# Two blocks on one core: the scan's keys on GpSimd, the residuals on VectorE, and the first feed-forward's output token-major

## The reference, cut to what matters

```python
def step(state, inp):                     # per head, chunkwise
    b = jnp.cumsum(gc, axis=2)
    o_inter = einsum('bhtk,bhkv->bhtv', qc * exp(b), state)
    decay = exp(minimum(b[:, :, :, None, :] - b[:, :, None, :, :], 0.0)) * mask
    scores = einsum('bhtk,bhsk,bhtsk->bhts', qc, kc, decay)
    o_intra = einsum('bhts,bhsv->bhtv', scores, vc)
...
x = x + rms_norm(mix, norm_mix_post[l])
h2 = rms_norm(x, norm_ffn_pre[l])
ff = (silu(h2 @ w_gate) * (h2 @ w_up)) @ w_down          # 2816 hidden
x = x + rms_norm(ff, norm_ffn_post[l])
x = x + (p[l] @ w_ple) * sigmoid(x @ w_ple_gate)
```

## Time and profile before

| what | value |
|---|---|
| median of 3 runs | 925.89 us (925.7 to 927.39) |
| the profiled execution's own time | 928.56 us |
| its span, first to last instruction | 926.7 us |
| mean granted TensorE clock | 0.978 |
| busy: PE / DVE / ACT / POOL | 95% / 64% / 48% / 5% of the span |
| read from memory | 141.87 MB |

### The profile page before, as it was taken

One profiled execution on the slowest core, in us unless ns is written; L12 is line 12 of the kernel. 1 busy time (PEld: TensorE's weight loads), 2 busy tenths in 40 slices (PEclk: granted clock), 3 DMA queues, 4 the chain that ended last, 5 costly groups with the idle time before them and its releaser, 6 DMA issues. The chain is left out here.

```text
span 926.7 us, 15775 instructions
## 1 busy us (share of the span) xinstructions
PE 882.5 (95%) x6990; PEld 860.9 (93%) x6990; DVE 597.2 (64%) x717; ACT 449.3 (48%) x524; POOL 44.4 (5%) x47
## 2 busy tenths in 40 slices
PE   5999989899999989999999999989996899999998
PEld 4999977899999989999999989988996899999997
DVE  5866975697576577555555577676776665555554
ACT  6577744345343664434343554464553644444441
POOL 1000000000000020000000021000342000000000
PEclk9999999899999999999999999998998999999999
DMA  9544323144445535555555526542231255555551
GB/s 341 195 152 168 122 105 136 46 139 139 144 141 181 184 132 182 182 182 182 182 183 183 181 95 229 168 157 95 92 119 60 91 182 182 182 182 182 182 183 46
DMA packets 21124, 143.94 MB, mean 155 GB/s; under 512 B 2579, under 2 KB 2595, under 8 KB 4417
## 3 DMA queue, kind: packets, MB, share of 16 engines
q1 hardware_dynamic: 20016, 139.51, 43.5%
q0 software_dynamic: 1040, 3.43, 1.1%
HBM read 141.87 MB, written 1.06 MB: 154 GB/s over the span
## 5 line engine op out<-in xcount | busy, mean ns | idle before, releaser
L1470 PE MATMUL ps<-xh,whi 128*128 128x256 f32 x1960 | 563.6, 288 | 18.3 <-issue 6.8
L1471 PE MATMUL ps<-xl,whi 128*128 128x256 f32 x1960 | 558.6, 285 | 0.0
L1472 PE MATMUL ps<-xh,wlo 128*128 128x256 f32 x1960 | 558.4, 285 | 0.0
L1470 PEld LDWEIGHTS ps<-xh,whi 128*128 128x128 f32 x1960 | 380.2, 194 | 21.9 <-issue 20.3
L790 DVE TENSOR_TENSOR wlo<-raw,whi 128x2048 fp32r<-128x2048 f32 x130 | 297.4, 2290 | 129.6 <-ACT whi L391 128.8
L1471 PEld LDWEIGHTS ps<-xl,whi 128*128 128x128 f32 x1960 | 380.2, 194 | 0.0
L1472 PEld LDWEIGHTS ps<-xh,wlo 128*128 128x128 f32 x1960 | 380.1, 194 | 0.0
L391 ACT ACTIVATE whi<-raw 128x2048 fp32r<-128x2048 f32 x130 | 247.9, 1908 | 163.6 <-DMA raw<-w 163.4
L574 ACT ACTIVATE xh<-work 128x512 fp32r<-128x512 f32 x27 | 17.1, 632 | 75.9 <-DVE work L1096 39.8
L1625 PE MATMUL ps<-work 128*128 128x128 f32 x224 | 32.3, 303 | 8.3 <-ACT work L471 8.3
L1625 PEld LDWEIGHTS ps<-work 128*128 128x128 f32 x224 | 30.2, 210 | 10.0 <-ACT work L471 9.9
(11 more groups left out here) (242 smaller groups left out, 666.3 us busy)
## 6 DMA issues: line engine op xcount, KB each, us to landing
raw<-w SPq DMA_DIRECT2D x130, 1024.0 KB, 4.9
x<-xT SPq DMA_DIRECT2D x2, 512.0 KB, 6.4
raw<-w SPq DMA_DIRECT2D x2, 512.0 KB, 7.5
work<-bias_scratch POOLq DMA_DIRECT2D x1, 1024.0 KB, 6.2
out<-x SPq DMA_DIRECT2D x4, 256.0 KB, 2.3
work<-lnr POOLq DMA_DIRECT2D x1, 512.0 KB, 6.0
work<-sgw POOLq DMA_DIRECT2D x1, 512.0 KB, 6.7
lvl_s<-lvl POOLq DMA_DIRECT2D x1, 448.0 KB, 8.3
```

The lines of the kernel that those rows point to most:

```text
L1470: mm(out, hi, xh[:, tile, :], start=start, stop=False, skip_group_check=skip)
L1471: mm(out, hi, xl[:, tile, :], start=False, stop=False, skip_group_check=skip)
L1472: return mm(out, wlo[:, slot, at:at + width], xh[:, tile, :], start=False, stop=stop, skip_group_check=skip)
```

## The change

The steps of the scan are put in two tables, `inside` (between the two halves of a unit) and `behind` (after a unit). K's half of `tree_update` goes to GpSimd as `keys_update`; ScalarE's copy waits for it. GpSimd's residual additions go to VectorE. `first_unit` makes the products with xh as soon as xh is there, and those with xl after. The down units of the first feed-forward accumulate token-major; their norm is taken per token (ScalarE's accumulated squares, factor by a power on GpSimd, a diagonal matrix on VectorE), and a product with that diagonal scales and turns them back to channels; VectorE adds them with the gain to x in one operation a tile. The folds, statistics and broadcast of n4 go.

```diff
 def hgrn_schedule():
-    steps = {}
-    for g, first in enumerate((10, 18)):
-        for lv in range(9):
-            steps.setdefault(first + lv, []).append(("level", g, lv))
-    for g, u in enumerate((19, 27)):
-        steps.setdefault(u, []).insert(0, ("pv", g, 0))
-    return steps
+    inside = {11: [("level", 0, 0)], 20: [("pv", 0, 0)], 28: [("pv", 1, 0)]}
+    behind = {18: [("level", 0, 8), ("level", 1, 0)], 27: [("level", 1, 8)]}
+    for lv in range(1, 8):
+        behind[10 + lv] = [("level", 0, lv)]
+        behind[19 + lv] = [("level", 1, lv)]
+    return inside, behind
...
 # GpSimd, ahead of the load of pT
+            def keys_update(g, lv):
+                half = 1 << (lv - 1)
+                n = 4 * T // (2 * half)
+                if lv == 1:
+                    pool.wait_ge(sem(f"q_init{g}"), 2)
+                else:
+                    pool.wait_ge(sem(f"decay{g}"), 2 * lv - 2)
+                pool.wait_ge(sem("Kc"), 7 * g + lv)
+                for d in range(2):
+                    pair = decay(g, d, lv - 1).rearrange("p (n two) -> p n two", two=2)
+                    v = G[g]["K"][d].rearrange("p h (n two w) -> p (h n) two w", two=2, w=half)[:, :, d, :]
+                    ins = nc.gpsimd.tensor_tensor(v, v, pair[:, :, 1 - d:2 - d].broadcast_to([P, n, half]), ALU.mult)
...
+                ins.then_inc(sem(f"ktree{g}"), 1)
+            for g in range(2):
+                for lv in range(1, 8):
+                    keys_update(g, lv)
...
-            for k in range(1, 4):
-                residual("n2", k)
...
-            for k in range(1, 4):
-                residual("ff", k)
...
+            for t in range(2):
+                pool.wait_ge(sem("ff_eps"), t + 1)
+                nc.gpsimd.tensor_tensor(fffac[:, t:t + 1], ffvar[:, t:t + 1], half_s[:, 0:1], ALU.pow).then_inc(sem("ff_fac"), 1)
...
 # ScalarE
                 if lv > 1:
-                    act.wait_ge(sem(f"tree{g}"), lv - 1)
+                    act.wait_ge(sem(f"ktree{g}"), lv - 1)
+                    act.wait_ge(sem(f"lv_mm{g}"), lv)
...
                 if kind == "pv":
                     act.wait_ge(sem(f"pv_mm{g}"), 1)
+                    if g == 0:
+                        both_ways(1, 1)
...
-                ahead(u)
+                if not U_ZI <= u < U_GA:
+                    ahead(u)
...
                             evac(u - 1 + s, zi[:, s, half * 512:half * 512 + 512], ACT.Copy, scale=rtok[:, 0, s:s + 1])
+                    ahead(u)
...
-                A(sq2[:, 2 * b:2 * b + 2, :], two(ps[3 + b][:, :]), ACT.Square).then_inc(sem("norm_sq"), 1)
-                for t in range(2):
-                    ins = A(mix[:, 2 * b + t, :], ps[3 + b][:, t * T:(t + 1) * T], ACT.Copy, scale=col("ffn_post", 2 * b + t))
-                ins.then_inc(sem("ff_copy"), 1)
+                A(ysq[:, b, :], ps[3 + b][:, :], ACT.Square, accum_out=ffsum[:, b:b + 1]).then_inc(sem("norm_sq"), 1)
...
 # VectorE, tree_update: Q alone, then the decays of the next level, each with a signal
+                for d in range(2):
+                    v = G[g]["Q"][d].rearrange("p h (n two w) -> p (h n) two w", two=2, w=half)[:, :, 1 - d, :]
+                    last = V.tensor_tensor(v, v, pairs[d][:, :, d:d + 1].broadcast_to([P, n, half]), ALU.mult)
...
-                if U_Q[0] <= u < U_ZI and (u - 4) % 6 == 5:
-                    gates((u - 4) // 6, 1, 1)
-                    if u < U_Q[1]:
-                        hgrn_dve("prep", 0, 0)
-                for step in steps.get(u, ()):
+                if u == U_Q[1] - 1:
+                    gates(0, 1, 1)
+                    hgrn_dve("prep", 0, 0)
+                for step in behind.get(u, ()):
                     hgrn_dve(*step)
                 ahead(u)
+                if u == U_ZI - 1:
+                    gates(1, 1, 1)
...
 # VectorE, n2
-                if k == 0:
-                    dve.wait_ge(sem("n2_y"), 1)
-                    V.tensor_tensor(x[:, t, :], x[:, t, :], tmp2[:, t, :], ALU.add).then_inc(sem("n2_x"), 1)
-                if k >= 2:
-                    gained_lo("n3", "ffn_pre", 8, k - 2)
-            gained_lo("n3", "ffn_pre", 8, 2)
+                dve.wait_ge(sem("n2_y"), k + 1)
+                V.tensor_tensor(x[:, t, :], x[:, t, :], tmp2[:, t, :], ALU.add).then_inc(sem("n2_x"), 1)
+                if k:
+                    gained_lo("n3", "ffn_pre", 8, k - 1)
...
 # VectorE, n4
+            def token_copy(b):
+                dve.wait_ge(sem("norm_sq"), before("sq", "n4") + b + 1)
+                V.tensor_copy(ytok[:, b // 2, (b % 2) * 512:(b % 2 + 1) * 512], ps[3 + b][:, :]).then_inc(sem("ff_copy"), 1)
+            def token_mean(t):
+                dve.wait_ge(sem("norm_sq"), before("sq", "n4") + 2 * t + 2)
+                link(V.tensor_tensor(ffvar[:, t:t + 1], ffsum[:, 2 * t:2 * t + 1], ffsum[:, 2 * t + 1:2 * t + 2], ALU.add))
+                V.tensor_scalar(ffvar[:, t:t + 1], ffvar[:, t:t + 1], 1.0 / D, EPS, ALU.mult, ALU.add).then_inc(sem("ff_eps"), 1)
+            def token_diag(t):
+                dve.wait_ge(sem("ff_fac"), t + 1)
+                V.tensor_scalar(diag[:, t, :], ident, fffac[:, t:t + 1], None, ALU.mult).then_inc(sem("ff_diag"), 1)
+            def token_residual(m):
+                if m % 2 == 0:
+                    dve.wait_ge(sem("ff_turned"), m // 2 + 1)
+                V.scalar_tensor_tensor(x[:, m, :], ps[TURNED[m // 2]][:, (m % 2) * T:(m % 2 + 1) * T], col("ffn_post", m),
+                                       x[:, m, :], ALU.mult, ALU.add).then_inc(sem("ff_x"), 1)
+            token_copy(0); token_mean(0); token_copy(1); token_diag(0)
+            token_copy(2); token_mean(1); token_copy(3); token_diag(1)
+            for k in range(4):
+                token_residual(2 * k)
+                token_residual(2 * k + 1)
+                if k:
+                    x_lo(k - 1)
+            x_lo(3)
...
 # TensorE, first_unit
+                for pair in range(4):
+                    blocks = [(m, k) for k in (2 * pair, 2 * pair + 1) for m in range(2)]
+                    pe.wait_ge(sem("act_hi"), before("hi", x_name) + pair + 1)
...
+                    pe.wait_ge(sem("act_lo"), before("lo", x_name) + pair + 1)
...
 # TensorE, the first feed-forward's output
+            def token_down(slot, base, s, c, kk, first, end):
+                xs = slice(s * P, (s + 1) * P)
+                wc = slice(1024 * kk + 512 * c, 1024 * kk + 512 * c + 512)
+                o = ps[3 + 2 * s + c][:, :]
+                mm(o, xh[:, base + kk, xs], whi[:, slot, wc], start=first, stop=False, skip_group_check=True)
+                mm(o, xl[:, base + kk, xs], whi[:, slot, wc], start=False, stop=False, skip_group_check=True)
+                return mm(o, xh[:, base + kk, xs], wlo[:, slot, wc], start=False, stop=end, skip_group_check=True)
...
-            last_down((U_PG - 1) % SLOTS, 2 * ((PAIRS1 - 1) % 2), "ff_bank")
-            idle_products(0, 14)
-            norm_stats("n4", sq2)
-            idle_products(0, 5)
-            norm_bc("n4")
-            idle_products(0, 9)
...
+            def turned(s, m):
+                return mm(ps[TURNED[m // 2]][:, (m % 2) * T + s * P:(m % 2) * T + (s + 1) * P], ytok[:, s, m * P:(m + 1) * P],
+                          diag[:, s, :], start=True, stop=True)
+            pe.wait_ge(sem("ff_copy"), 2)
+            pe.wait_ge(sem("ff_diag"), 1)
+            for m in range(8):
+                turned(0, m)
+            idle_products(2, 5)
+            pe.wait_ge(sem("ff_copy"), 4)
+            pe.wait_ge(sem("ff_diag"), 2)
+            for m in range(8):
+                last = turned(1, m)
+                if m % 2:
+                    last.then_inc(sem("ff_turned"), 1)
+            idle_products(2, 6)
```

151 lines of the change are left out of this document (74 added, 77 removed).

## The result

The changed kernel takes **902.2 us** (median of 4 runs, 900.72 to 903.32) against 926.64 for the kernel before on the same chip: ratio 0.9714, 95% interval 0.9683 to 0.9745, so 2.9% faster. Its profiled execution took 901.93 (span 900.1, mean granted clock 0.988), that of before 928.56 (926.7, 0.978).

The account below looks back on a forecast made before the run. TensorE, busy 95% of the span, was taken as the bound. Gains 16 + 3.5 + 5.5 + 1.5 + 0.9 = 27.4 us off the profiled 928.56 gave 901.2, as a median 898.5 us, range 893 to 909.

Parts of the forecast that it names:

- Parts 1 and 2: Scan: reordered levels, copies and splits, plus key updates moved to GpSimd, gain 16 us (bounds: 19.6, loss of about 4).
- 19.6 us lost: Scan: its 153.9 us less a sum of 134.3 us at TensorE's pace, taken as the time lost.
- Key updates at 1.48: Scan: GpSimd's price per key update, taken from its residual additions; at most one hold of VectorE per level.
- one of my own signs for "wrong": Scan: levels over 7.6 us apart (units 20-26), key updates over 2 us, or VectorE's times up over 20 us in all.
- Part 3: First feed-forward: eleven token-major down units at 5.43 instead of 5.77 us, gain 3.5 us (bounds 3 and 4.5).
- Part 4: Tail of the first feed-forward: shorter chain from last down product to next unit, gain 5.5 us (3.5 to 6.5).
- Part 5: Second residual and first_unit: gain 1.5 us (0 to 2) at the second norm, 0.9 us at the sixth.
- (a): Scan: shared port holds VectorE a second time in about half of levels 2-7; gain 6, median 908.5; chance 0.17.
- (b): Scan: both key updates of every level hold VectorE through the shared port, about 929 us; chance 0.05.
- (c): First feed-forward: token-major pays only 0.8 us instead of 3.5, median 901; chance 0.05.
- (d): Feed-forward tail: diagonal and turned products arrive no earlier, gain 0 instead of 5.5, median 904; chance 0.06.
- (e): Scan: another engine, ScalarE's queue in units 12 to 15, paces it as before; within 2 us of 925.9; chance 0.02.

Follow-up runs that it names:

- the second comparison: The changed kernel itself, unedited, run a second time beside the kernel before on the same chip: 901.0 us, ratio 0.9703.
- the run with the waits out: Changed kernel with ScalarE's first copies, VectorE's first group-1 query products and the last hidden products reordered to remove three waits: 898.62 us.
- the channel-major run: Changed kernel with the first feed-forward's down projections, norm and residual as before; scan and attention output residual as changed: 908.31 us.
- The doubled keys: Changed kernel with each GpSimd key update followed by a second in-place operation of the same shape (times one): 908.42 us.

## Why the prediction was right

It said 898.5 with 893 to 909, faster; it came to 902.2. By medians the gain is 24.4 us here (926.64 to 902.2) and 27.3 in the second comparison (928.31 to 901.0), for a forecast of 27.4. By its steps:

- **Parts 1 and 2**, gain 16: measured 14.4, and 15.0 in the second profile. The waits at level 6 and ahead of (1,1) went as said, (0,8) was 0.5 late where I had said 1. About 3.7 of the 14.4 are clock (an estimate: before, level (0,6) and the unit behind it took 1.4 and 0.3 us longer with part of them at clock 0.5, (1,1) and its unit 0.9 and 1.1). The "19.6 us lost" was too high: with unit 28 its sum at pace is 140.1, and the run with the waits out, where TensorE never waits, took 143.48. The sum left out 2.0 us of the longer first and second tree levels and the 0.08 us that each first product behind a level takes more (0.20 for 0.12, 0.31 for 0.23). So 17.1 could be had, and the 3.5 us that the prediction left standing are about this floor. What is missing up to 17.1 is the 0.5 at (0,8) and a wait that I hadn't seen, at (0,1): 2.1 us behind one activation on ScalarE. I looked for what stood behind ScalarE's new waits, not at what its copies stood behind.
- **Key updates at 1.48**: median 1.52, mean 2.00, so one of my own signs for "wrong" (over 2 us) was reached, by a hair, and said nothing. GpSimd's duration holds its own waiting for VectorE. The right sign was the other one, VectorE's growth: against the run with the keys on VectorE five gates 0.72 longer in the mean and the 128x1024 products 1.8 in all, 5.4 us, not 20. Another sign of mine failed too: levels (1,1) to (1,2) and (1,2) to (1,3) are 8.41 and 7.68 apart, over 7.6, by the longer products of these levels and not by a wait. And no split went above 2.29, since each one that meets a key update had begun before it.
- **Part 3**, 3.5: measured 2.36. A token-major unit took 5.47 and not 5.43, since its first products start 0.23 to 0.24 us apart (0.30 x 10 and 0.25 for the last unit), and the last wait grew by 0.88. I had allowed for 0.2. Not all of the 0.88 is due to the shorter unit: in the seven profiles with the changed feed-forward the wait is 1.1 to 1.6 us, and the channel-major run has 1.07. Run "waits out" shows the cause: a split for a later unit stood ahead of the last hidden products.
- **Part 4**, 5.5: measured 5.39; TensorE's unit starts 5.94 behind the last down product, I had 5.8, with the idle products last as said. But the channel-major run splits it: 3.35 are the token-major tail's, the other 2.04 came with `first_unit` alone, and about 1.7 of those are clock.
- **Part 5**, 1.5 and 0.9: measured 0.76 and 2.4. At the second norm I added two edits that remove the same wait. At the sixth the wait was sized right (0.9) and the lower clock behind it, which I had called unchanged, went too (1.5).
- **What no step held**: clock. The head statistics ran 1.6 us slower than before, and rest, less the sixth norm, 2.5 faster, in code that is the same; +0.9 in sum.

The steps missed by -1.6, -1.1, -0.1, -0.7 and +1.5, and the clock added 0.9: that their sum came so near is partly luck.

The sum was 27.4 against a profile's own 928.56, so 901.2; the changed kernel's profile took 901.93. What put the median 3.7 us off is the step behind the sum: I took off another 2.67 because the profiled execution lay so far above the median of three runs. That excess wasn't a property of the profile. With a fourth run the kernel before had a median of 926.64, and in three later comparisons 927.91, 927.26 and 928.31: the 925.89 was a low draw.

The rivals: (a) and (b) ask for VectorE to be held. The doubled keys show that it happens, 0.50 us a query update, and the changed kernel's levels at 7.54 show that it costs nothing there, though VectorE's times grew by 5.4 us in all. (c) is out: a unit gained 0.30 us, and 0.227 is the pace of 512 columns. (The 0.07 us a unit that the prediction works out for (c) comes to 0.06, so (c) stood for 0.7 us in all and the rows for five times that, not four.) (d) is out, (e) too: TensorE is busy 144.04 of 146.20 us in the scan.

## What to carry to other kernels

Two edits that shorten the same wait don't add: measure each alone before pricing the pair (17.5 for 14.4 in the scan, 0.51 and 0.76 for 0.76 at a norm). Where totals scatter by 2 us, cut both traces at the same products and compare stage by stage; a stage that no edit touches then shows what the clock does by itself. A run in which the engine never waits gives the pace of a stretch; a sum of single instructions came out 3.4 us under it here. Work given to GpSimd was cheap here where it fell on VectorE's waits, its PSUM reads and splits already begun, so look at when it will run, not only for how long.

## What the runs showed of the hardware that I had not expected

- **Who holds whom.** In the changed kernel a key update takes 1.04 us at the least and up to 3.41 when a split is in progress, about the split's 2.29 more; the splits stay at 2.28 to 2.30, 130 of 130. A gate clamp that starts during a key update takes 1.28 to 1.37 instead of 0.43 (four cases), in the run with the keys twice a query update up to 1.64 instead of 0.69. The simplest reading of who waits is that the one that began first keeps the port. All twelve splits that overlap a key update in the changed kernel had begun first, so it alone can't tell this from "a split never waits". The three runs with the waits out can: in each, one split starts during a key update, and it takes 3.02 us. In the first of them:

```profile
81.15 2.28 DVE L819 TENSOR_TENSOR wlo<-raw,whi 128x2048 fp32r<-128x2048 f32 x1
81.31 3.51 POOL L350 TENSOR_TENSOR work<-work 128x512 f32<-128x512 f32 x1 [56.25 <-DVE work L966]
83.35 0.68 DVE L878 TENSOR_TENSOR work<-ps,bcs 128x512 f32<-128x512 f32 x1
83.95 3.02 DVE L819 TENSOR_TENSOR wlo<-raw,whi 128x2048 fp32r<-128x2048 f32 x1
```

The update waits for the first split and then holds the second; the product that reads PSUM between them keeps its 0.68. The Trainium skill's "SBUF — State Buffer" (SBUF: two separate sides) states it as a rule, for a VectorE instruction with two SBUF inputs or in a two-port mode and one of GpSimd: whichever of the two starts first gets the pair of ports for its whole instruction. The trace agrees in each of the cases above. By that rule GpSimd's duration holds its wait, which is why a mean of 2.00 us meant nothing for VectorE.
- **The clock as scatter.** "rest" is the same program in ten profiles (all but that of before and that with the old first unit): 343.1 to 343.8 us with 13.7 us at half clock, 344.4 to 345.4 with 17.1, 347.3 to 347.4 with 20.5. That is 4 us, twice what a measurement here should tell from nothing, and a large part of the scatter between runs. What decides it I can't say; the runs differ ahead of the stretch by shifts of a few us.
